# Fewer modulation chunks ahead of the experts, columns taken as they come, and one root for two row tiles, in a two-block transformer kernel

## What is computed

```python
# block 1
h = rmsnorm(x, g_attn_norm);  proj = h @ w_in            # pool part, q and kv latents, rope part
y_pool = pool_mixer(u, w_pool, ...)                      # causal means over 2, 4, 8, 16 rows, per group
y_attn = mla_attention(q_lat, kv_lat, k_r, ...)          # 8 heads
x = x + concat(rmsnorm(y_pool, g_out_pool), rmsnorm(y_attn, g_out_attn)) @ w_out
h = rmsnorm(x, g_ffn_norm)
logits = h @ w_router + b_router                         # 32 experts, top 4, softmax over the 4
x = x + sum over the 4 experts of gate * (clipped_swiglu(h @ w_gate_up[e] + b) @ w_down[e] + b)
x = rmsnorm(x, g_final)
# block 2
mod = silu(c) @ w_ada + b_ada                            # 6 * 1024 numbers: sh1, sc1, g1, sh2, sc2, g2
hn = rms(x, norm1_g) * (1 + sc1) + sh1;  proj = hn @ w_in_2
y = concat(fox (6 heads), mLSTM (4 heads), moba (6 heads) of proj)
x = x + g1 * (y @ w_out_2)
hn = rms(x, norm2_g) * (1 + sc2) + sh2
gate, up = split(hn @ w_gate_up_2);  x = x + g2 * ((silu(gate) * up) @ w_down_2)
```

## Time and profile before

| | us |
|---|---|
| median of 3 runs (range) | 1465.42 (1463.99 to 1467.93) |
| profiled execution, own time | 1465.46 |
| its span | 1463.6 |
| TensorE busy | 1409.3 (96% of the span) |
| VectorE, ScalarE, GpSimd busy | 410.1, 225.0, 21.9 |
| moved by DMA | 497 MB, 339 GB/s over the span |
| mean granted TensorE clock | 0.996 of full |

### The profile page before, as it was taken

One profiled execution on the slowest core, in us unless ns is written; L12 is line 12 of the kernel. 1 busy time (PEld: TensorE's weight loads), 2 busy tenths in 40 slices (PEclk: granted clock), 3 DMA queues, 4 the chain that ended last, 5 costly groups with the idle time before them and its releaser, 6 DMA issues.

```text
span 1463.6 us, 17945 instructions
## 1 busy us (share of the span) xinstructions
PE 1409.3 (96%) x7194; PEld 753.7 (51%) x7194; DVE 410.1 (28%) x1021; ACT 225.0 (15%) x425; POOL 21.9 (1%) x14
## 2 busy tenths in 40 slices
PE   6998999999999999999999999999899998999999
PEld 5654444444444444344334433443388864888843
DVE  5546311211211111121112111211325563001784
ACT  1332111111111111011101110111123442100000
POOL 3200000000000000000000000000000000000000
PEclk9999999999999999999999999999999999999999
DMA  9978999999999999999999999999994326444400
GB/s 340 354 294 345 413 428 428 428 429 429 428 429 428 429 429 429 428 428 429 429 429 428 428 429 429 429 428 429 415 362 169 115 87 201 141 147 145 160 12 29
DMA packets 83777, 497.05 MB, mean 340 GB/s; under 512 B 6285, under 2 KB 47962, under 8 KB 56762
## 3 DMA queue, kind: packets, MB, share of 16 engines
q1 hardware_dynamic: 83132, 495.46, 83.4%
q10 hardware_dynamic: 606, 1.06, 0.2%
HBM read 495.44 MB, written 1.05 MB: 339 GB/s over the span
## 4 chain that ended last, share of the span: by engine, by line
PE 74%; DMA 21%; DVE 2%; ACT 1%; issue 1%; SPq 0%; DVEq 0%; ACTq 0%
PE PS L955 19%; DMA ring<-in_w_gate_up_dram 13%; PE PS L981 11%; PE PS L1329 11%; DMA qk<-in_w_gate_up_dram 8%; PE PS L940 6%; PE PS L1084 6%; PE PS L1339 5%; PE PS L989 3%; PE PS L773 2%; PE PS L670 2%; PE PS L1208 2%; PE PS L967 1%; PE PS L949 1%; PE PS L962 1%
## 5 line engine op out<-in xcount | busy, mean ns | idle before, releaser
L955 PE MATMUL PS<-ring,store 128*64 128x512 f32 x1360 | 301.0, 594 | 14.0 <-DMA ring<-in_w_gate_up_dram 13.7
L955 PEld LDWEIGHTS PS<-ring,store 128*64 128x64 f32 x1360 | 94.4, 137 | 207.9 <-issue 170.7
L2073 DVE TENSOR_SCALAR store<-PS 128x512 f32<-128x512 f32 x32 | 22.1, 691 | 619.7 <-PE PS L955 619.7
L1329 PE MATMUL PS<-xc,ring 128*128 128x256 f32 x704 | 155.3, 384 | 2.3 <-DVE xc L1769 2.3
L981 PE MATMUL PS<-ring,store 128*64 128x512 f32 x704 | 154.8, 592 | 0.0
L1329 PEld LDWEIGHTS PS<-xc,ring 128*128 128x128 f32 x704 | 135.8, 193 | 21.9 <-DVE xc L1769 2.5
L940 PE MATMUL PS<-store,rows 128*128 128x64 f32 x1056 | 125.2, 272 | 1.3 <-DVE store L2051 1.3
L940 PEld LDWEIGHTS PS<-store,rows 128*128 128x128 f32 x1056 | 123.4, 192 | 2.1 <-issue 2.1
L981 PEld LDWEIGHTS PS<-ring,store 128*64 128x64 f32 x704 | 49.3, 137 | 90.7 <-issue 89.1
L1084 PE MATMUL PS<-ring,xc 128*128 128x240 f32 (+1 forms) x448 | 93.6, 366 | 0.0
L1499 ACT ACTIVATE store<-store 128x512 f32<-128x512 f32 x32 | 20.1, 629 | 452.5 <-DVE store L2073 452.5
(11 more groups left out here) (367 smaller groups left out, 1219.3 us busy)
## 6 DMA issues: line engine op xcount, KB each, us to landing
ring<-in_w_gate_up_dram SPq DMA_DIRECT2D x85, 2048.0 KB, 35.0
ring<-in_w_down_dram SPq DMA_DIRECT2D x44, 2048.0 KB, 37.3
qk<-in_w_gate_up_dram SPq DMA_DIRECT2D x21, 2048.0 KB, 37.5
ring<-in_w_ada_dram SPq DMA_DIRECT2D x24, 1024.0 KB, 15.3
store<-in_w_gate_up_dram SPq DMA_DIRECT2D x11, 2048.0 KB, 34.9
ring<-in_w_gate_up_dram SPq DMA_DIRECT2D x22, 1024.0 KB, 5.1
xc<-in_w_down_dram SPq DMA_DIRECT2D x10, 2048.0 KB, 36.5
store<-in_w_down_dram SPq DMA_DIRECT2D x10, 2048.0 KB, 37.8
```

Source lines behind the costliest of these rows:

```text
L955: mm = pe.matmul(bank(b)[CAP * h:CAP * (h + 1), :], xg[:, k, :], w[:, b * FE + h * 512:b * FE + (h + 1) * 512], start=False, stop=(k == KD ...
L1329: mm = pe.matmul(bank(4 + 2 * (j % 2) + up)[:, f * T:(f + 1) * T], chunk(n)[:, k, f * P:(f + 1) * P], cols[:, k, :], start=(k == 0), stop= ...
```

## The change

- Chunk order: two ada chunks instead of six ahead of the experts, six instead of eight behind them, and six between the in2 chunks (two after in2(0), two after in2(6, 0), two after in2(8, 1)). The segments of the modulation and the places of `turn_mod` and `keep_mod` follow. The number of w_out_2's first chunk stays 428, that of the first chunk after the experts goes from 406 to 402. VectorE's written order around `scale_weights` stays.
- Columns: the first chunk after each of three norms takes the tiles in the order 0, 4, 1, 5, 2, 6, 3, 7, each when its copy is there.
- `square_sums`: VectorE adds the four parts, TensorE sums with one matmul for each row tile; the first is placed later.
- FFN norm: x is turned as it is added, unscaled; the router's weights are multiplied by the gain ahead of time, and 1/rms is applied to the logits. ScalarE scales the rows. The pick for the gather stands ahead of the gates, two `add_x` between gather and expert 0, `turn_mod(0)` inside expert 0.
- Norms 1 and 2: one root for both row tiles, tile 0 scaled by VectorE and tile 1 by ScalarE. At norm 2 both tiles' sums are added first.
- The band matmul of the pool is split at the band's edge. The bias of the modulation is loaded as six single rows, later, instead of six broadcasts over 32 rows. Layout of q and k columns and of the experts' buffers is changed so that two weight thirds can be loaded earlier, one in halves.

```diff
-ADA_SEGMENTS = (0, 6, 8, 12, 16, 20, 24)
-ADA_BANK = (7, 1, 2, 0, 1, 5)
+ADA_SEGMENTS = (0, 6, 8, 16, 18, 20, 24)
+ADA_BANK = (7, 7, 0, 1, 3, 5)
...
-N_MOE = N_OUT1B + 2 + 6
+N_MOE = N_OUT1B + 2 + 2
...
-N_IN2 = N_AFTER + 8
+N_IN2 = N_AFTER + 6
...
-N_OUT2 = N_IN2 + len(IN2_CHUNKS)
+N_OUT2 = N_IN2 + len(IN2_CHUNKS) + 6
...
-          *range(N_AFTER, N_IN2), *range(N_OUT2 + 4, N_GU2)]
+          *range(N_AFTER, N_IN2), *(N_IN2 + i for i in (1, 2, 8, 9, 13, 14)), *range(N_OUT2 + 4, N_GU2)]
...
+def n_in2(c):
+
+    return N_IN2 + c + 2 * sum(c >= first for first in (1, R_GATES, 9))
...
-            def square_sums(squares):
-
+            def square_sums(n):
+
+                pe.wait_ge(sig["sq_reduced"], n)
                 for t in range(NT):
-                    for f in range(4):
-                        mm = pe.matmul(bank(3 if squares is pool_sq else 0)[:, t:t + 1], squares[:, f, t * P:(t + 1) * P],
-                                       ones[:, 0:1], start=(f == 0), stop=(f == 3))
+                    mm = pe.matmul(bank((3, 0)[n - 1])[:, t:t + 1], sq_cols[:, t * P:(t + 1) * P],
+                                   ones[:, 0:1], start=True, stop=True)
                 mm.then_inc(sig["pool_sum"], 1)
...
-            for i in range(6, 10):
-                ada(i)
-            turn_scaled()
-            ada(10)
-            ada(11)
+            turned[0] += 1
+
...
-            for i in range(12, 18):
+            for i in range(8, 14):
                 ada(i)
             pe.wait_ge(sig["z_ready"], 4)
-            pe.wait_ge(sig["x_squared"], 9)
-            turn_rows(8, base=4)
-            ada(18)
-            ada(19)
-            need_cols()
+            pe.wait_ge(sig["x_squared"], 8)
+            turn_rows(("rows_ready", 5), ("rows_act", 3), base=4)
...
                 if c == 0:
+                    ada(14)
+                    ada(15)
+                if c == 1:
                     turn_mod(1, 7)
-                    turn_mod(2, 6)
-                if c == 1:
-                    pe.wait_ge(sig["mod_cols"], 3)
+                if c == 2:
+                    pe.wait_ge(sig["mod_cols"], 2)
                     spread(1, 0, (6, 7))
             pe.wait_ge(sig["bcast_kept"], 1)
             turn_soft(0, 6)
             turn_soft(1, 7)
             in2(6, 0)
+            ada(16)
+            ada(17)
             pe.wait_ge(sig["heads_cols"], 1)
...
             in2(8, 1)
+            ada(18)
+            ada(19)
             turn_probs(0)
...
-            for t in range(NT):
-                at = slice(t, t + 1)
-                dve.wait_ge(sig["x_squared"], 2 * t + 8)
-                do.step(v.scalar_tensor_tensor(out=mean_x[:, at], in0=halves_x[:, 2 * t:2 * t + 1], scalar=EPS,
-                                               in1=halves_x[:, 2 * t + 1:2 * t + 2], op0=ALU.add, op1=ALU.add))
-                do.step(v.scalar_tensor_tensor(out=mean_z[:, at], in0=mean_x[:, at], scalar=EPS, in1=mean_z[:, at],
-                                               op0=ALU.mult, op1=ALU.add))
-                rsqrt_column(both[:, at], mean_z[:, at], rsqrt_tmp[:, at])
-                do.tell(v.tensor_scalar(rows[:, t, :], rows[:, t, :], both[:, at], RSQRT_SCALE, ALU.mult, ALU.mult),
-                        "rows_ready")
+            do.step(v.tensor_tensor_reduce(out=gate_b, in0=rows[:, 0, :], in1=rows[:, 0, :], scale=1.0 / D, scalar=0.0,
+                                           op0=ALU.mult, op1=ALU.add, accum_out=mean_z[:, 0:1]))
+            dve.wait_ge(sig["x_squared"], 8)
...
+            rsqrt(both, mean_z, rsqrt_tmp[:, 0:NT], "rows_ready")
+            do.tell(v.tensor_scalar(rows[:, 0, :], rows[:, 0, :], both[:, 0:1], None, ALU.mult), "rows_ready")
...
+            act.wait_ge(sig["rows_ready"], 7)
+            do.tell(nc.scalar.activation(rows[:, 1, :], x_sb[:, 1, :], ACT.Copy, scale=stat(rs, S_NORM2)[:, 1:2]),
+                    "rows_act")
...
             for t in range(NT):
                 add_product(4, t, "gate_used", 1, N_OUT2 + 4)
-                dve.wait_ge(sig["x_squared"], 10 + 2 * t + 2)
-                at = slice(2 * t, 2 * t + 1)
-                do.step(v.scalar_tensor_tensor(out=st[:, at], in0=st[:, at], scalar=EPS,
-                                               in1=st[:, 2 * t + 1:2 * t + 2], op0=ALU.add, op1=ALU.add))
-                rsqrt_column(r_[:, at], st[:, at], rsqrt_tmp[:, at])
-                do.tell(v.tensor_scalar(rows[:, t, :], x_sb[:, t, :], r_[:, at], RSQRT_SCALE, ALU.mult, ALU.mult),
-                        "rows_ready")
+            dve.wait_ge(sig["x_squared"], 13)
+            do.step(v.scalar_tensor_tensor(out=mean, in0=st[:, 0:4:2], scalar=EPS, in1=st[:, 1:4:2],
+                                           op0=ALU.add, op1=ALU.add))
+            rsqrt(r_, mean, rsqrt_tmp[:, 0:NT], "rows_ready")
+            do.tell(v.tensor_scalar(rows[:, 0, :], x_sb[:, 0, :], r_[:, 0:1], None, ALU.mult), "rows_ready")
```

More of the change, by code:

```diff
@@ L317, in two_blocks @@
[L317 to L322, removed]
-        top = work[:, 4432:4448].rearrange("p (t e) -> p t e", t=NT)
-        logit_parts = work[:, 4736:4736 + T]
@@ L329, in two_blocks @@
+        gexp = moe[:, 4512:4576].rearrange("p (t e) -> p t e", t=NT)
+        small = moe[:, 4576:4704]
+        lr_row, list_f = moe[0:1, 4992:5088], moe[0:1, 5088:5136]
         list_eq, list_w = (pt[0:1, i, :].rearrange("p (j i) -> p j i", j=4) for i in range(2))
-        diag = work[:, 5136:5392].rearrange("p (t n) -> p t n", t=NT)
-        third = [qk[:, :, :].rearrange("p a b -> p (a b)"), xc[:, :], store[:, WORK + 2 * D - 2 * SLOT:WORK + 2 * D]]
+        third = [qk[:, :, :].rearrange("p a b -> p (a b)"), xc[:, :], store[:, 0:2 * SLOT]]
@@ L377, in two_blocks, with in2_bank @@
         SEVEN_TAIL = 3
+        def in2_bank(c):
+            return 4 + c % 2 if c else 3
         def slot(n):
@@ L668, in project @@
                     for t in range(NT):
-                        for k in range(KD):
+                        for i, k in enumerate(COLS):
+                            if (c, t) == (0, 0):
+                                need_col(k)
                             mm = pe.matmul(bank(b)[:, t * w:(t + 1) * w], cols[:, k, t * P:(t + 1) * P],
-                                           chunk(n)[:, k, :], start=(k == 0), stop=(k == KD - 1))
+                                           chunk(n)[:, k, :], start=(i == 0), stop=(i == KD - 1))
                     mm.then_inc(chunk_used, 1)
@@ L927, in _ @@
             add_x(4)
+            ada(6)
             pe.wait_ge(sig["routed"], 1)
@@ L1944, in add_part, with reduce_squares @@
                                                op0=ALU.mult, op1=ALU.add), told)
+            def reduce_squares(squares):
+                do.tell(v.tensor_reduce(sq_cols, squares.rearrange("p f t -> p t f"), AX.X, ALU.add), "sq_reduced")
             heads_1 = list(attention_heads(1))
@@ L1982, in _ @@
                     add_part(4, t, h, r_att, "x_added")
+            for b in (0, 1):
+                dve.wait_ge(sig["rows_turned"], 4 + b + 1)
+                do.tell(v.tensor_copy(cols[:, 2 * b:2 * b + 2, :], bank(b).rearrange("p (k t) -> p k t", k=2)), "cols_dve")
+            turned[0] += 1
             dve.wait_ge(sig["x_squared"], 4)
```

336 lines of the change are left out of this document (185 added, 151 removed).

## The result

| | before | changed |
|---|---|---|
| median of runs, us (range) | 1466.68 (1463.99 to 1467.93, 4 runs) | 1482.08 (1476.29 to 1484.62, 4 runs) |
| ratio, 95% interval | | 1.0102 (1.0068 to 1.0136) |
| profiled execution, own time | 1465.46 | 1476.29 |
| its span | 1463.6 | 1474.5 |

The forecast was 1468.0 with a range of 1460 to 1475: no change was the likeliest, and the kernel is slower beyond the range. The profiled execution of the changed kernel was the fastest of its four, so two questions follow: where 10.9 us of span went, and why the other runs take 5 to 8 us more.

A forecast was written before the change was run, and what follows sets the result against it. Weights bound the experts; around them, a serial path through TensorE, VectorE and ScalarE. −10.9 + 17.0 + 1.0 − 6.3 = +0.8, with clock +2.4, on 1465.46 gives 1467.9, taken as 1468.0 us; range 1460 to 1475.

The forecast's parts named there:

- What bounds the experts: Experts run at the pace of their weights, so their end moves with expert 0's start: −10.9 us (−9.4 to −12.4).
- Start and FFN norm to expert 0: Ahead of the experts: −2.8 us by attention's end, −8.85 from FFN norm to expert 0, together −11.65.
- nothing on the path waits for: At the start, replacing six ada bias broadcasts by later single rows costs 0 us, between −1 and +0.3.
- Norm 1: Behind the experts, one root and ada chunks out of the way let in2(0) start 3.8 us earlier.
- The stall: VectorE's wait for w_out2 loads delays gates and TensorE: +17.0 us from MoE's end (+13 to +20), +20.8 from in2(0).
- the second stop: Within the stall, TensorE waits some 3 us more behind the scaling of load 430; clock loss afterwards +1.0 us.
- the landing's two prices: For w_out2 loads: 5.1 us taken from the rows (shortest 4.9, median 6.1), against the skill's estimate of 4.4.
- Between the pairs and output products: Between attention pairs, two ada chunks and a turned modulation add +1.0 us (+0.5 to +1.5).
- Norm 2: First gate-up product of block 2 3.2 us earlier, its first 64 at full clock: −6.3 us (−3.3 to −6.6).
- the half clock after every stop: Rival: TensorE at half clock after each stop, 3.4 us at each of the stall's two, 2.0 before expert 0; 1472.8; chance 0.24.
- The stall isn't there: Rival: loads 428 to 431 land by the time VectorE asks, so no stall; 1448.5 us; chance 0.10.
- the clock that I had put aside: Allowance for TensorE's clock after uncounted stops: +0.6 us ahead of expert 0, +1.0 after the stall's second wait.

The follow-up runs named there:

- e7: Changed kernel with only GpSimd's second bias split held back until TensorE has turned the first heads; 1480.08 us, ratio 1.0088.
- e10: Changed kernel run again with no edit, which gave its second profile; 1480.52 us, ratio 1.0073.
- e8: Kernel before with norm 2's part alone (both tiles added first, one root, two engines scaling), columns still waited for together; 1465.04 us, ratio 0.9984.
- e1: Changed kernel with 164 satisfied waits (82 words) ahead of TensorE's first instruction; 1484.63 us, ratio 1.0131.
- e9: Changed kernel with output-weight scalings where VectorE is idle, GpSimd's second bias split held back, 82 wait words ahead of the expert loop; 1456.98 us, ratio 0.9916.
- e4: e3 with e1's waits ahead of TensorE's first instruction; 1467.71 us, ratio 0.9995.
- e12: e11 with the first pass of TensorE's expert loop written out; 1452.43 us, ratio 0.9885.
- e3: Changed kernel with VectorE's four output-weight scalings moved behind the bias rows (two) and between the convolution channels (two); 1464.46 us, ratio 0.9977.
- e2: Kernel before with 348 satisfied waits (174 words) ahead of TensorE's first instruction; 1498.02 us, ratio 1.0232.
- e5: e3 with GpSimd's second bias split held back until TensorE has turned the first heads; 1459.32 us, ratio 0.9943.
- e6: e5 with 32 words of satisfied TensorE waits right ahead of the expert loop; 1461.55 us, ratio 0.9962.
- e11: e9 without its 82 wait words; 1456.46 us, ratio 0.9916.
- e13: e11 run once more, on the same chip as e12; 1455.97 us, ratio 0.9913.

## Why the prediction was wrong, step by step

- **What bounds the experts**: right. 911.6 and 912.0 us, and the end moved by −10.0 for −10.9.
- **Start and FFN norm to expert 0**: −10.4 for −11.65 in the first profile, and −3.4 in the second. The step that failed is "nothing on the path waits for" the broadcasts: 0, between −1 and +0.3. I asked who waits for the moved loads and not who stands behind them in the queue. b_down did, and GpSimd behind it. VectorE's rope ops (2.56 us undisturbed) take 2.7 us more in the first profile and 5.3 more in the second; of that TensorE's path pays 0.5 and 3.0, and in the second half clock follows. The first addition of w_out's product is at 107.96 for 110.29, −2.3 for my −2.8, so short by as much as that wait; the other 0.8 of the miss lies in the FFN norm.
- **The 5.8 us between the median and the first profiled run**: my range had no place for them, and their cause stays open. The second profile has 2.5 of its 8.4 us by the rope ops. But e7, without them, has the median of e10 within 0.5 us, so they don't make the difference of the medians. What is left is a later start and the clock behind short stops, which differ from run to run in e8 too.
- **Norm 1**: −3.8 forecast, +1.6 measured, the largest miss. The norm's own steps were priced right: without the gap e1 and e9 take 13.8 us there for 17.5 before, −3.7, and e4 and e12 14.9 and 15.0, where half clock falls on the turning of the rows just ahead of in2(0) (3.4 and 3.5 us for 2.3 and 1.9). What failed is that I priced work and waits and left out the code: 4.88 us of fetching behind the jump. Nothing in the trace before shows it, since there its block had been fetched during the loop; no bound of mine covered it.
- **The stall**: right in kind and close in size, +22.3 for +20.8. The transposes came 17.55 us after in2(5) (forecast 17.4), the load that the second stop waits for (w_out_2's third chunk) took 6.40 us to land instead of 5.1, and half clock ran over 1109.4 to 1123.0, in which TensorE had 5.23 us of work and so lost 2.6 (taken 2.3). The second stop lowered the clock too (1137 to 1140), 1.5 us at least for my 1.0. Of the landing's two prices the row's was the nearer. The Trainium skill, "DMA: Bandwidth & Descriptors", section "Anatomy of one DMA — SWDGE (gpsimd) path", gives an estimate of 4.4 us, and the trace does not agree: 4.96 and 6.40. These loads are SyncE's (queue q1, "hardware_dynamic"), and that section is on the path by GpSimd.
- **Between the pairs and output products**: +1.2 for +1.0, and another +1.7 up to the last output product that I did not have, with a stretch at half clock from 1215.2 to 1218.6. It is behind a stop of 1.58 us. The kernel before and e3 have the same stop, of 1.57 and 1.59 us, at full clock and 42.7 us in that stretch, and so have all versions without the stall; e1, e7 and e10, which have the stall, have half clock there and 44.3 to 44.4. Why the clock falls in these alone stays open.
- **Norm 2**: right, −5.8 for −6.3, the clock included. In e8 one root alone gives 2.2.
- **The rivals**: the half clock after every stop was partly so, but its 1472.8 is not why the kernel is slow: at the stall's two stops some 4.1 us were lost of the 6.8 it held. "The stall isn't there" is what e3 makes, and there the kernel has 1464.5 rather than 1448.5, since e3 has the two other faults and its own. With all of them mended e12 comes to 1452.4.
- **The sum**: 2.4 forecast and 10.9 measured in the profile. Norm 1 with the gap accounts for 5.4, the start 1.25, the stall 1.5, the output products 1.7, four other stretches +0.2, +0.3, +0.2 and −0.1, the experts −0.35; that is 10.1, less 1.6 of the clock that I had put aside. A further 5.8 us lie between this profile and the median. Without the 5.4 of the code the profiled run would have been at 1471 and inside the range; the median of 1482 would not.

## What to carry to other kernels

When a chunk order is changed, write for each load the product that frees its slot, and look at which engine waits for it in a fixed order and what stands behind that wait; here moving four multiplications of 2.29 us back in one engine's order gave 17.6 us. A load that is made smaller moves all that stand behind it in its queue, and the engine that they release can meet another one: ask for each moved landing what it starts, and price it by what the critical engine then waits (0.5 and 3.0 us here), not by what the disturbed engine takes. A path through a loop and a jump has a price that depends on where the code lies; compare the row with "issue" at a loop's exit in each version before believing a difference of 5 us.

## What the runs showed of the hardware that was not expected

- Behind the jump out of a loop TensorE stood 4.88 to 5.09 us in nine profiles (the changed kernel twice, e2, e3, e5, e6, e7, e11 and e13), each time with a 16 KB block of code landing in the gap, and not at all in the kernel before, e1, e4, e8, e9 and e12, where one more block had come late in the loop's first pass (at 270 us in the kernel before, where the changed kernel's last one came at 245). In e1, e4 and e9 a shift of 82 words removed it, 32 words in e6 did not, and 174 brought it into the kernel before.
- A satisfied wait is not free on TensorE: a word of two waits takes 0.108 to 0.110 us in its queue, in e9 (82 words, 8.9 us), e6 (32, 3.5 us), e1 (82, 8.7 us) and e2 (174, 18.7 us). How much of it shows depends on how far the queue is ahead of the products: nothing in e6, 4.84 us in e9, 16.4 at the start of e2.
- Two VectorE ops on 256 columns that take 0.76 us took 3.40 to 3.50 beside GpSimd's ops in three profiles (the changed kernel's two and e3's), so a landing that moves by 4 us changes the time of another engine by 3 to 5. TensorE waited 0.5, 3.0 and 3.6 us for it.
- TensorE's clock came down to half behind, or at the end of, every stop of 3 us or more that follows the first columns in these profiles. Behind stops of 1 to 2 us it did so in some runs and not in others (1.34 and 1.01 us ahead of the experts: six profiles with half clock, among them e10 and e7, and the first profile without). In e12, whose longest stop from the start of the column products on is 1.7 us, 3.4 us of half clock are left ahead of the end.
